# Handing the output projection to the MLP on chip, and spreading work inside the samples' recurrence

## The reference

```python
# rwkv_mixer, per token: S = S*w + (S @ -kk) (kk*a)^T + v k^T ; y = S r
def step(S, inp):
    r_t, w_t, k_t, v_t, kk_t, a_t = inp
    sa = jnp.einsum('nhij,nhj->nhi', S, -kk_t)
    S = S * w_t[:, :, None, :] + sa[..., None] * (kk_t * a_t)[:, :, None, :] + v_t[..., None] * k_t[:, :, None, :]
    return S, jnp.einsum('nhij,nhj->nhi', S, r_t)
...
mix = jnp.concatenate([oa, ob, oc], axis=-1)            # the three head groups
x = x + jnp.einsum('nlc,cd->nld', mix, w['w_out'])      # output projection
u = jnp.einsum('nld,df->nlf', rmsnorm(x, w['norm2_g']), w['mlp_up'])
x = x + jnp.einsum('nlf,fd->nld', jnp.square(jax.nn.relu(u)), w['mlp_down'])
```

## Time and profile before

| | |
|---|---|
| median of 3 runs | 3264.35 us (3263.09 to 3264.71) |
| the profiled execution, its time | 3269.89 us |
| the profiled execution, its span | 3268.1 us |
| PE busy | 3056.9 us, 94% of the span |
| DVE, ACT, POOL busy | 48%, 25%, 11% |
| mean granted clock of PE | 0.966 |
| samples' recurrence in the trace | about 1492 to 1561 us |
| output projection | about 1561 to 1773 us |
| MLP | from 1773.6 us |

### The profile page before, as it was taken

The page is one execution under the profiler, slowest core; times in us unless marked ns, Lnnn a source line. Parts: engine busy times, 40 slices in busy tenths (PEclk is TensorE's granted clock), DMA queues, the critical chain, the costliest instruction groups (busy, mean ns, idle before and its releaser), DMA issues. The chain is left out here.

```text
span 3268.1 us, 65648 instructions
## 1 busy us (share of the span) xinstructions
PE 3056.9 (94%) x27080; PEld 2594.3 (79%) x27080; DVE 1571.2 (48%) x3052; ACT 817.4 (25%) x1506; POOL 350.9 (11%) x473
## 2 busy tenths in 40 slices
PE   7999999799788898885997999999999999999998
PEld 7999998466477777784785888888888998888887
DVE  6211121577565666654334444444446445444545
ACT  5000000465423233322233211122113221122112
POOL 4000000454233223310000000000000000000000
PEclk9999999899899999996998999999999999999999
DMA  4122121523222230002455310111114201110111
GB/s 152 70 73 70 69 85 48 152 83 102 72 88 83 96 107 25 22 13 73 147 177 170 125 49 28 51 51 51 51 48 156 89 26 51 51 51 26 51 45 66
DMA packets 144827, 248.84 MB, mean 76 GB/s; under 512 B 21536, under 2 KB 100896, under 8 KB 144096
## 3 DMA queue, kind: packets, MB, share of 16 engines
q1 hardware_dynamic: 144608, 245.68, 22.5%
HBM read 185.12 MB, written 60.52 MB: 75 GB/s over the span
## 5 line engine op out<-in xcount | busy, mean ns | idle before, releaser
L2757 DVE TENSOR_TENSOR m_y<-m_y,m_db 128x512 f32<-128x512 f32 x512 | 351.3, 687 | 323.4 <-PE m_db L2526 323.1
L2524 PE MATMUL m_ub<-m_hh,m_wuh 128*128 128x352 f32 (+1 forms) x1280 | 452.4, 353 | 17.5 <-DVE m_hl L2703 17.4
L2525 PE MATMUL m_ub<-m_hl,m_wuh 128*128 128x352 f32 (+1 forms) x1280 | 450.6, 352 | 0.0
L2526 PE MATMUL m_ub<-m_hh,m_wul 128*128 128x352 f32 (+1 forms) x1280 | 450.0, 352 | 0.0
L2524 PE MATMUL m_db<-m_wdh,m_uh 128*128 128x512 f32 x1024 | 406.8, 397 | 4.8 <-DVE m_wdl L2712 4.7
L2526 PE MATMUL m_db<-m_wdh,m_ul 128*128 128x512 f32 x1024 | 403.8, 394 | 0.0
L2525 PE MATMUL m_db<-m_wdl,m_uh 128*128 128x512 f32 x1024 | 402.6, 393 | 0.0
L183 PE MATMUL p_bank<-p_xh,p_wh 128*128 128x416 f32 x800 | 286.4, 358 | 11.6 <-DVE p_wl L304 11.6
L184 PE MATMUL p_bank<-p_xl,p_wh 128*128 128x416 f32 x800 | 284.0, 355 | 0.0
L185 PE MATMUL p_bank<-p_xh,p_wl 128*128 128x416 f32 x800 | 283.0, 354 | 0.0
L2524 PEld LDWEIGHTS m_ub<-m_hh,m_wuh 128*128 128x128 f32 x1280 | 241.4, 189 | 46.0 <-issue 12.5
(11 more groups left out here) (393 smaller groups left out, 5022.0 us busy)
## 6 DMA issues: line engine op xcount, KB each, us to landing
m_wur<-w_up SPq DMA_DIRECT2D x64, 512.0 KB, 6.0
m_wdr<-w_dn SPq DMA_DIRECT2D x64, 512.0 KB, 4.1
p_ring<-units SPq DMA_DIRECT2D x30, 768.0 KB, 6.1
out_projT<-p_ob SPq DMA_DIRECT2D x100, 208.0 KB, 1.9
cp_z<-out_projT SPq DMA_DIRECT2D x8, 1408.0 KB, 7.9
p_wr<-w_fm SPq DMA_DIRECT2D x20, 512.0 KB, 3.6
p_mix<-mixT SPq DMA_DIRECT2D x16, 512.0 KB, 5.0
p_x<-x SPq DMA_DIRECT2D x16, 512.0 KB, 3.6
```

Source lines behind the costliest of these rows:

```text
L2524: pe.matmul(out, wh, mh, start=first, stop=False)
L2525: pe.matmul(out, wh, ml, start=False, stop=False)
L2526: return pe.matmul(out, wl, mh, start=False, stop=last)
L2757: dve.tensor_tensor(yh, yh, db[(2 * a + h) % ND][:, :], ALU.add).then_inc(y_added, 1)
```

## The change

Four things are changed.

1. The tiles of the output projection come in another order (`out_tiles`): prompt rows 1024 to 2047 first, then the samples, then prompt rows 0 to 1023 (the "near" tiles, from tile index `near0` = 9). The 9 far tiles go to `h2T` in HBM as before. The 8 near tiles go from the transposes in PSUM straight to `m_hh` and `m_hl` (`Handoff.keep_high` on ACT, `keep_low` on DVE), with no store to `h2T` and no load of it.
2. The last near tile's residual, norm, transposes and splitting, and the splitting of the one before, are issued in the MLP's block. Buffers and PSUM banks are shared by both blocks, and the first block of `w_up` is loaded and split during the projection.
3. On PE in the samples' recurrence the 48 products of queries and state are spread: 2 heads at step 5, 1 after step 9, 1 after the first masks' products, 2 in `special`. `state_rows` does 1 head in `levels_of` and 5 in `special`.
4. On DVE the low parts of the output weights are spread: `low(0, 2)` in `levels_of`, `low(2, 5)` after `vm`, `low(5, KC)` after the recurrence's output is stored away.

```diff
@@ tensor_walk
+            def state_queries(n):
+                for _ in range(n):
+                    p, h = queries.pop(0)
+                    for b in range(NB):
+                        e.matmul(y_bank(half(h), p, NQ * b, NQ), S0[half(h), 0, p, b, :],
+                                 ar_[0][half(h), p, 0, 1, NQ * b:NQ * (b + 1)], start=(p == 0 and b == 0), stop=False)
...
-                    for p, h in heads(NP3):
-                        for b in range(NB):
-                            e.matmul(y_bank(half(h), p, NQ * b, NQ), S0[half(h), 0, p, b, :],
-                                     ar_[0][half(h), p, 0, 1, NQ * b:NQ * (b + 1)], start=(p == 0 and b == 0), stop=False)
+                    state_queries(2)
...
-                    state_rows(heads(NP3)[0:2])
+                    state_rows(heads(NP3)[0:1])
...
-                state_rows(heads(NP3)[2:])
+                state_queries(2)
+                state_rows(heads(NP3)[1:])
@@ vector_walk
+                    low(5, KC)
                     if sample:
                         state_end()
...
                 W_(G, ("tt2", g), seg)
+                low(0, 2)
...
-                    if ahead and not isinstance(e, Rehearsal):
-                        for k in range(0, 5) if name == "vm" else range(5, KC):
-                            ahead.low(e, k)
+                    if name == "vm":
+                        low(2, 5)
@@ new functions
+def out_tiles():
+
+    half = SEQ // 2 // P
+    return [(P * i, P) for i in range(half, 2 * half)] + [(SEQ, NS)] + [(P * i, P) for i in range(half)]
...
+    def turn(self, pe, t):
+        n = self.tiles[t][1]
+        pe.wait_ge(self.scaled, t + 1)
+        if t > self.near0:
+            pe.wait_ge(self.kept_low, 2 * (t - self.near0))
+        elif t:
+            pe.wait_ge(self.h_out, t)
...
+    def keep_high(self, act, t):
+        act.wait_ge(self.turned, t + 1)
+        for i in range(2):
+            for k, j, c in self.part(t, i):
+                a = act.activation(self.hh[:, k, c], self.tp[i][:, j, :], ACT.Copy, scale=self.g[:, k:k + 1])
+            a.then_inc(self.kept_high, 1)
...
+    def keep_low(self, dve, t):
+        for i in range(2):
+            dve.wait_ge(self.kept_high, 2 * (t - self.near0) + i + 1)
+            for k, j, c in self.part(t, i):
+                a = dve.scalar_tensor_tensor(out=self.hl[:, k, c], in0=self.tp[i][:, j, :], scalar=self.g[:, k:k + 1],
+                                             in1=self.hh[:, k, c].bitcast(F32), op0=ALU.mult, op1=ALU.subtract)
+            a.then_inc(self.kept_low, 1)
@@ out_project, scalar (the vector engine alike: add, invert, keep_low or copy_out)
+            for t in range(NT - 1):
+                if t:
                     high_m(t + 1)
+                hand.norm(act, t)
+                if t == near0 + 1:
+                    act.wait_ge(hand.consts_in, 32)
+                if t > near0:
+                    hand.keep_high(act, t - 1)
+                if t == near0:
+                    act.wait_ge(hand.wu_in[0], 16)
+                    act.activation(hand.wuh0[:, :, :], hand.wur[:, 0], ACT.Copy).then_inc(hand.wu_high, 1)
@@ mlp, sync
-            sp.dma_start(wur[:, 0], w_up[0]).then_inc(wu_in[0], 16)
-            load_h(first, 0)
-            sp.dma_start(wur[:, 1], w_up[1]).then_inc(wu_in[1], 16)
-            for k in range(1, NR):
-                load_h(first, k)
-            for k in range(NR, KC):
-                load_h(first, k)
             for j in range(2):
                 sp.dma_start(wdr[:, j], w_dn[j]).then_inc(wd_in[j], 16)
-            sp.wait_ge(h_low, KC)
-            for a in range(NT):
+            hand.store_x(sp, hand.NT - 1)
+            for a in range(NT - 1):
                 sp.dma_start(y[:, a, :], x2[P * a:P * a + P, :]).then_inc(y_in, 16)
+            sp.wait_ge(hand.x_stored[0], 16 * ((hand.NT + 1) // 2))
+            sp.dma_start(y[:, NT - 1, :], x2[P * (NT - 1):P * NT, :]).then_inc(y_in, 16)
+            sp.wait_ge(hand.turned, hand.NT)
@@ mlp, tensor
+                        if start and j == 0 and not H.index:
+                            if g:
+                                hand.turn(pe, hand.NT - 1)
+                            else:
+                                hand.turn(pe, hand.NT - 2)
+                                pe.wait_ge(hand.kept_low, NT)
                         for k in range(KC):
-                            if start and j == 0 and g == 0:
-                                pe.wait_ge(h_low, H.index * KC + k + 1)
+                            if start and j == 0 and H.index and g == 0:
+                                pe.wait_ge(h_low, k + 1)
+                            if start and j == 0 and not H.index and g and k % 4 == 0:
+                                pe.wait_ge(hand.kept_low, 2 * NT - 1 + k // 4)
@@ mlp, scalar (the vector engine alike: add, invert, keep_low twice)
-            high_up(first, 0, 0, None)
-            for k in range(KC):
-                high_h(first, k)
+            hand.norm(act, hand.NT - 1)
+            hand.keep_high(act, hand.NT - 2)
+            hand.keep_high(act, hand.NT - 1)
```

More of the change, by code:

```diff
@@ L77, in project @@
         with ExitStack() as start:
-            xs = [start.enter_context(nc.sbuf_tensor(f"p1_xs{i}", [P, KH, TG], F32)) for i in range(NX)]
-            part = start.enter_context(nc.sbuf_tensor("p1_part", [P, TG], F32))
+            xs = [start.enter_context(nc.sbuf_tensor(f"p1_xs{i}", [P, KH, TG], F32, side="left")) for i in range(NX)]
+            part = start.enter_context(nc.sbuf_tensor("p1_part", [P, TG], F32, side="left"))
         wvh = s.sb("p1_wvh", [P, KC, NV], F32R)
@@ L1701, in vector_walk, with low @@
             ct = lambda ap: ap.rearrange("p (c t) -> p c t", t=C)
+            def low(k0, k1):
+                if ahead and not isinstance(e, Rehearsal):
+                    for k in range(k0, k1):
+                        ahead.low(e, k)
             def rho(seg):
@@ L2197, in out_project @@
+def out_project(nc, outer, ahead, hand, xtok, w_up, h2T):
+    NT, near0, tiles = hand.NT, hand.near0, hand.tiles
     with ExitStack() as ctx:
         s = Scope(nc, ctx, outer)
-        wh, wl, m, mh, ml = ahead.wh, ahead.wl, ahead.m, ahead.mh, ahead.ml
+        wh, wl, m, mh, ml, mixT = ahead.wh, ahead.wl, ahead.m, ahead.mh, ahead.ml, ahead.mixT
         w_low, mix_in, m_high, m_low = ahead.w_low, ahead.mix_in, ahead.m_high, ahead.m_low
-        g = s.sb("p5_g", [P, KC])
-        idt = s.sb("p5_ident", [P, P])
@@ L2365, in super_loop, with mlp @@
     body(NSUP - 1)
-def mlp(nc, outer, h2T, x2, w_up, w_dn, fg, sel, y_out):
+def mlp(nc, outer, hand, h2T, x2, w_up, w_dn, fg, sel, y_out):
     W = SEQ // 2 + NS
@@ L2404, in mlp @@
         st = s.sb(n_("stat"), [P, 3, NT + 1])
-        ub = [s.ps(n_(f"ub{i}"), [P, 512]) for i in range(3)]
-        db = [s.ps(n_(f"db{i}"), [P, 512]) for i in range(ND)]
-        tb = s.ps(n_("tb"), [P, 512])
+        ub = [hand.bank[i] for i in (6, 7, 4)]
+        db, tb = hand.bank[0:ND], hand.bank[5]
         h_in = [s.sem(n_(f"h_in{i}")) for i in range(NR)]
@@ new lines, in decoder_trunk @@
+    with (Era(nc) as outer, Era(nc) as base, Era(nc) as first, ExitStack() as common, ExitStack() as ring,
+          ExitStack() as kept, ExitStack() as across):
+        project(nc, first, A["xT"], A["g1"], A["cst_ones"], A["w_fm"], A["w_v"], A["projT"], A["vtok"])
+        shared = RwkvShared(nc, common, base, cst, wts, zc)
+        prompt_attention(nc, first, A["projT"], A["vtok"], A["cst_mask_w"], A["cst_mask_0"], A["sinks"],
+                         A["cst_ident"], mixT, shared)
+        early = SampleEarly(nc, ring, base, cst, zc, A["shift0"], A["state0"])
+        with ExitStack() as inside:
+            side = SampleAttention(nc, inside, outer, early, A["projT"], A["vtok"], A["units"], A["cst_mask_b"],
+                                   A["cst_mask_a"], A["sink_a"], A["cst_ident"], mixT)
+            rwkv(nc, outer, "cp", False, zc, shared, early, mixC, 0, A["state_p"], side, stale=first)
+        first.close()
+        ahead = OutWeights(nc, kept, outer, mixT, A["w_o"])
+        with ExitStack() as raw:
+            ahead.staging(nc, raw, outer)
+            rwkv(nc, outer, "cs", True, zc, shared, early, mixC, SEQ, A["state_s"], ahead=ahead)
+        ring.close()
+        common.close()
+        hand = Handoff(nc, across, outer, A["g2"], A["cst_ident"], x2)
+        out_project(nc, outer, ahead, hand, A["x"], A["w_up"], h2T)
+        kept.close()
+        mlp(nc, outer, hand, h2T, x2, A["w_up"], A["w_dn"], A["fg"], A["cst_sel"], A["y"])
```

281 lines of the change are left out of this document (147 added, 134 removed).

## The result

The changed kernel takes 3244.58 us (median of 4 runs, 3242.68 to 3246.40); the kernel before took 3264.53 beside it (3263.09 to 3273.89). The ratio is 0.9928, 95% interval 0.9913 to 0.9943: some 23.5 us faster by it (18.6 to 28.4 by its interval; the two medians differ by 19.95). The time is slower than the 3231.5 forecast and than the range's upper end of 3241.

What follows compares the result with a forecast made beforehand. PE was taken as nearly always busy, so only its stands or half clock could give time. Seam 24.1 plus recurrence 8.7 made 32.8 us off the profiled 3269.89, or 3231.5 us against the median of 3264.35; range 3224 to 3241.

Steps and rivals of the forecast that it cites:

- The seam: From the projection's last products to the end of the MLP's second group: 43.5 us shrinks to 19.4, giving 24.1 us.
- the clock's loss: At the seam, PE's products run slower after its stands; 1.5 us booked once.
- The fetch rival: The branch into the MLP stalls PE for an instruction fetch, at least 1.6 us: 3234 to 3236; chance 0.15.
- Near tiles: In the projection, the last low part comes some 2.5 us later, 2.7 us of spare stay: no cost.
- the slower rival: ACT and DVE contend on their shared PSUM bank; from 0.86 us a step slower than before; chance 0.05.
- The recurrence: In the samples' recurrence, spread queries, rows and low parts let `cs_S` begin at 1544.8 instead of 1553.54: 8.7 us.
- Ahead of the right-hand side two heads of queries (2.8) and five of rows (3.18 / 4 = 0.8 each, 4.0): In the samples' recurrence, this PE work replaces 3.18 us: 3.6 us more, leaving -1.7.
- 2 us less: Recurrence bound: rows and queries ahead of the right-hand side all at half-clock price (5 x 1.21) leave 6.7 us.

## Why the prediction was wrong, step by step

**The seam: right.** 24.7 against 24.1. The single prices held: ACT's small parts 2.15 / 8 = 0.27 (0.28 forecast), DVE's 0.27 (0.29), stands of 0.7 and 2.4 us (1.3 and 2.5), the clock's loss once. In all twelve traces with the new seam, 18.7 to 19.0 us lie between the start of the last product and the third group, where 43.7 lay before. The low clock shrinks from 34.1 us to 3.4; at half the rate that is 30.7 / 2 / 3245 = 0.0047 of mean clock, and the runs list 0.9658 and 0.9708.

**The fetch rival: not seen.** PE's transposes began 0.95 us behind the start of the last product, across the change of block, 0.6 of it on its own queue. That is less than the smallest landing (1.6) that the rival would have cost. The Trainium skill, "Runtime: NRT & Kernel Launch", section "Instruction fetch mechanics", lets a branch outside the fetched window stall; here no such stall appeared, and no run shows whether the target had been fetched.

**Near tiles: right.** No wait inside them; the small parts stayed at 0.27 us each while ACT and DVE read the same bank, so the slower rival did not occur. From `cs_S` to the last product's end lie 209.3 us in both traces.

**The recurrence: mechanism right, size wrong** (8.7 forecast; 3.4 between the two traces, 2.4 to 3.55 at equal clock). The step that failed is "Ahead of the right-hand side two heads of queries (2.8) and five of rows (3.18 / 4 = 0.8 each, 4.0)". The 3.18 of the earlier trace rows was measured at granted clock 1.00. At half clock a head of rows is 1.36 to 1.4: five took 6.80 and not 4.0. The bound "2 us less" priced a head at 1.21 and left out that the path behind it runs at half clock too. The old order hid this, since its bound was DVE's train.

Measured from the first `rw_hsum` product, the 5.3 us between 8.7 and 3.4 fall on four places.

- PE comes to the last queries 3.9 us earlier and not 5.3. One head of queries by itself took 1.79 from start to start and not 1.39, and one head of state rows by itself 1.76 and not 1.21. At half clock one, two and six heads of queries in a row took 1.79, 3.10 and 8.33, so each further piece costs 0.4 to 0.5.
- From there to the right-hand side the changed kernel takes 5.4 more than before and not 3.6; the two heads of queries there took 1.75 and not 2.8, because the clock was full just then, which gave back 1.05 of the 2.8 lost on rows.
- From the right-hand side to the end of the mean the half clock costs 1.9 more than before, for which the forecast had nothing.
- The last 0.3 lie behind `cs_yc`.

So `cs_yc` came 4.6 us earlier and not 9.6.

**The MLP's pitch: no term at all.** +4.3 us, by the addresses behind 608 bytes of small tiles. The range had nothing for it.

**The sum.** -24.7 - 3.5 + 4.3 = -23.9; measured by the ratio -23.5. That these agree to 0.4 is luck: the interval is 5 us wide to either side, and each stretch's clock varies. With the recurrence at 8.7 and no pitch the forecast would have held. The two profiled executions differ by 27.3, and this can be laid out without a rest: 6.4 ahead of the first `rw_hsum` product, where the code is the same; 3.4 in the recurrence; 24.7 at the seam; 7.2 lost in the MLP.

## What to carry to other kernels

Before pricing a product from a row, look up the clock in that row's window: a price from a stretch that was warm by luck doesn't hold for a stretch that is mostly cold. When a change moves allocations, list the start addresses of all of PE's operands modulo 128 before and after; small tiles in the middle shift all that comes behind them, and for long loops of fp32 products a pad is a cheap experiment. Two edits that remove the same wait are to be priced together.
